# Weight units of the expert stages loaded in pairs of 1 MB instead of singly at 512 KB

## The reference

```python
def peer_ffn(xn, w_peer_q, sub_keys, expert_u, expert_v):
    ...
    best, pick = lax.top_k(cand, PEER_TOPK)
    expert_idx = jnp.take_along_axis(cand_idx, pick, axis=-1)
    gates = jax.nn.softmax(best, axis=-1)
    ...
    def step(args):
        xc, ic, gc = args
        u = expert_u[ic]
        hval = jnp.einsum('cd,chkd->chk', xc, u).astype(jnp.float32)
        a = (gc * jax.nn.gelu(hval, approximate=False)).astype(xc.dtype)
        return jnp.einsum('chk,chkd->cd', a, expert_v[ic])
```

## Time and profile before

| | us |
|---|---|
| three runs: median (lowest to highest) | 1323.77 (1323.52 to 1325.63) |
| span of the profiled execution | 1321.3 |
| PE busy | 1298.0 |
| DVE busy | 1067.7 |
| ACT busy | 818.5 |
| POOL busy | 215.6 |

### The profile page before, as it was taken

The page is one execution under the profiler, slowest core; times in us unless marked ns, Lnnn a source line. Parts: engine busy times, 40 slices in busy tenths (PEclk is TensorE's granted clock), DMA queues, the critical chain, the costliest instruction groups (busy, mean ns, idle before and its releaser), DMA issues.

```text
span 1321.3 us, 21738 instructions
## 1 busy us (share of the span) xinstructions
PE 1298.0 (98%) x8066; PEld 1199.7 (91%) x8066; DVE 1067.7 (81%) x1964; ACT 818.5 (62%) x1601; POOL 215.6 (16%) x153
## 2 busy tenths in 40 slices
PE   8999999999999999999999989999999999999998
PEld 6998888888889888889999989999989999999995
DVE  6867776666777675778999779999988898999985
ACT  6886555555556555455677688888665555555553
POOL 3002030000000000000000010110233444654510
PEclk9999999999999999999999999999999999999999
DMA  6534366565535345654566755566688999999982
GB/s 228 179 122 136 112 225 191 189 186 190 184 131 174 128 144 176 223 197 144 192 215 201 231 199 200 202 209 209 235 291 311 353 383 351 356 377 363 356 275 93
DMA packets 83135, 292.73 MB, mean 222 GB/s; under 512 B 10749, under 2 KB 11405, under 8 KB 82774
## 3 DMA queue, kind: packets, MB, share of 16 engines
q1 hardware_dynamic: 68182, 239.65, 53.1%
q0 software_dynamic: 14848, 51.69, 11.0%
HBM read 288.95 MB, written 2.34 MB: 220 GB/s over the span
## 4 chain that ended last, share of the span: by engine, by line
PE 80%; DVE 9%; DMA 5%; ACT 4%; issue 2%; POOL 0%; SPq 0%; POOLq 0%; ACTq 0%; DVEq 0%
PE bank L2404 78%; DMA raw<-in_wts 4%; DVE wl L661 3%; DVE rows L1599 1%; ACT wh L1743 1%; PE bank L2502 1%; PE bank L2490 1%; DMA rows<-in_u_rows,pick 1%; DVE oi L1576 0%; ACT oi L2324 0%; DVE gates L1631 0%; DVE gates L1584 0%; DVE oj L1572 0%; ACT oi L2328 0%; DVE us L1590 0%
## 5 line engine op out<-in xcount | busy, mean ns | idle before, releaser
L2404 PE MATMUL bank<-hTb,wh 128*128 128x416 f32 (+3 forms) x2768 | 826.8, 363 | 5.4 <-DVE wl L661 3.8
L2404 PE MATMUL bank<-hTb,wl 128*128 128x208 f32 (+2 forms) x2584 | 651.9, 264 | 0.0
L661 DVE TENSOR_TENSOR wl<-raw,wh 128x1024 fp32r<-128x1024 f32 x429 | 522.4, 1224 | 134.5 <-ACT wh L1743 133.1
L1743 ACT ACTIVATE wh<-raw 128x1024 fp32r<-128x1024 f32 x429 | 449.4, 1056 | 207.7 <-PE bank L2404 113.9
L2404 PEld LDWEIGHTS bank<-hTb,wh 128*128 128x128 f32 (+1 forms) x2768 | 505.5, 188 | 28.7 <-issue 6.7
L2404 PEld LDWEIGHTS bank<-hTb,wl 128*128 128x128 f32 (+1 forms) x2584 | 492.0, 190 | 4.8
L2404 PE MATMUL bank<-wh,hTb 128*128 128x512 f32 (+2 forms) x552 | 175.0, 398 | 1.4 <-DVE hTb L695 1.4
L2404 PEld LDWEIGHTS bank<-wh,hTb 128*128 128x128 f32 (+1 forms) x552 | 102.1, 186 | 24.3 <-DVE wl L661 1.6
L641 POOL DMA_INDIRECT rows<-in_v_rows,pick x48 | 95.9, 1998 | 92.5 <-DVE acc L1610 80.7
L641 POOL DMA_INDIRECT rows<-in_u_rows,pick x48 | 71.5, 1489 | 235.9 <-DVE dots L1599 231.7
L2404 PE MATMUL bank<-wl,hTb 128*128 128x512 f32 (+2 forms) x276 | 100.3, 389 | 0.0
(11 more groups left out here) (429 smaller groups left out, 1403.0 us busy)
## 6 DMA issues: line engine op xcount, KB each, us to landing
raw<-in_wts SPq DMA_DIRECT2D x441, 512.0 KB, 4.3
x<-in_x SPq DMA_DIRECT2D x4, 256.0 KB, 6.9
sk<-in_sk SPq DMA_DIRECT2D x1, 1024.0 KB, 6.8
spill<-x SPq DMA_DIRECT2D x1, 1024.0 KB, 7.6
xr<-few_x POOLq DMA_DIRECT2D x2, 512.0 KB, 12.3
x<-spill SPq DMA_DIRECT2D x4, 256.0 KB, 7.4
rows<-in_u_rows,pick POOLq DMA_INDIRECT x48, 7.5
rows<-in_v_rows,pick POOLq DMA_INDIRECT x48, 8.2
```

The lines of the kernel that those rows point to most:

```text
L661: e.tensor_tensor(b[:, :], raw[u % RAW][:, :], a[:, :].bitcast(F), ALU.subtract).then_inc(S("lo"), 1)
L1743: e.activation(parts_of(u)[0][:, :], raw[u % RAW][:, :], ACT.Copy).then_inc(S("hi"), 1)
L2404: return e.matmul(o, l, r, start=first, stop=last, skip_group_check=True)
```

## The change

From the first even unit of U on (186) up to unit 439, two units travel in one transfer. The host lays them side by side, so that each of the 128 partitions gets 8 KB in one piece. These 254 units make 127 transfers. The four buffers become four quarters of one tile `raws`, so that a pair fills two neighbouring ones: units 4k+2 and 4k+3 in the second half, 4k and 4k+1 in the first. Units 0 to 185 and unit 440 are loaded as before.

A pair's transfer is issued when the low steps of both units that held the half before are done: for even u, `lo` at least u-2, which is the end of unit u-3's low step. Before, unit u waited for the end of unit u-4's, and unit u+1 for that of u-3. Both units' high steps wait for the landing of the whole pair, on the semaphore of its first quarter; a table `landed` holds which semaphore and which count.

```diff
+def paired(units):
+    first = units.index(("U", ORDER[0]))
+    first += first % 2
+    return first, first + (len(units) - first) // 2 * 2
...
+        PAIRS, SINGLE = paired(units)
+        landings = [0] * RAW
+        landed = []
+        for u in range(len(units)):
+            slot = u % RAW
+            if PAIRS <= u < SINGLE:
+                slot -= u % 2
+            if not (PAIRS <= u < SINGLE and u % 2):
+                landings[slot] += 16
+            landed.append((f"raw{slot}", landings[slot]))
...
-        raw = [sb(f"raw{i}", [128, 1024]) for i in range(RAW)]
+        raws = sb("raws", [128, RAW * 1024])
+        raw = [raws[:, two(1024, i)] for i in range(RAW)]
...
             def weights(n):
                 for u in range(loaded[0], n):
+                    if PAIRS <= u < SINGLE:
+                        if u % 2 == 0:
+                            e.wait_ge(S("lo"), u - RAW + 2)
+                            e.dma_start(raws[:, 1024 * (u % RAW):1024 * (u % RAW) + 2048],
+                                        I["pairs"][(u - PAIRS) // 2]).then_inc(S(landed[u][0]), 16)
+                        continue
                     if u >= RAW:
                         e.wait_ge(S("lo"), u - RAW + 1)
-                    e.dma_start(raw[u % RAW][:, :], I["wts"][u]).then_inc(S(f"raw{u % RAW}"), 16)
+                    e.dma_start(raw[u % RAW], I["wts"][u - max(0, u - PAIRS)]).then_inc(S(landed[u][0]), 16)
...
-                    e.wait_ge(S(f"raw{u % RAW}"), 16 * (u // RAW + 1))
+                    e.wait_ge(S(landed[u][0]), landed[u][1])
```

More of the change, by code:

```diff
@@ L654, in low @@
                     if units[u][1] == "w_ple_gate":
-                        e.scalar_tensor_tensor(out=wl[u % SPL][:, :], in0=raw[u % RAW][:, :],
+                        e.scalar_tensor_tensor(out=wl[u % SPL][:, :], in0=raw[u % RAW],
                                                scalar=gpc[:, units[u][2]:units[u][2] + 1],
@@ L660, in low @@
                     a, b = parts_of(u)
-                    e.tensor_tensor(b[:, :], raw[u % RAW][:, :], a[:, :].bitcast(F), ALU.subtract).then_inc(S("lo"), 1)
+                    e.tensor_tensor(b[:, :], raw[u % RAW], a[:, :].bitcast(F), ALU.subtract).then_inc(S("lo"), 1)
                 lows[0] = max(lows[0], n + 1)
@@ L1739, in high @@
                             e.wait_ge(S("in_later"), 96)
-                        e.activation(wh[u % SPL][:, :], raw[u % RAW][:, :], ACT.Copy,
+                        e.activation(wh[u % SPL][:, :], raw[u % RAW], ACT.Copy,
                                      scale=gpc[:, k:k + 1]).then_inc(S("hi"), 1)
                         continue
-                    e.activation(parts_of(u)[0][:, :], raw[u % RAW][:, :], ACT.Copy).then_inc(S("hi"), 1)
+                    e.activation(parts_of(u)[0][:, :], raw[u % RAW], ACT.Copy).then_inc(S("hi"), 1)
                 highs[0] = max(highs[0], n + 1)
@@ L3261, in layout @@
     rows = lambda v: np.ascontiguousarray(np.broadcast_to(v.reshape(1, -1), (128, v.size)))
-    k = {"wts": w, "x": a["x"], "p": a["p"]}
+    first, end = paired(units)
+    k = {"wts": np.concatenate([w[:first], w[end:]]), "x": a["x"], "p": a["p"]}
+    k["pairs"] = np.ascontiguousarray(w[first:end].reshape(-1, 2, 128, 1024).transpose(0, 2, 1, 3)).reshape(-1, 128, 2048)
     k["fold"] = np.zeros((128, 2, 128), np.float32)
```

## The result

The changed kernel took 1403.38 us (median of 4 runs, 1396.40 to 1404.48), the kernel before, run beside it, 1323.64 us (4 runs, 1322.85 to 1325.63). The ratio on record is 1.0578 (not quite the quotient of the two medians, 1.0602), with a 95% interval of 1.0553 to 1.0604: **80 us slower**, where 21.5 us had been forecast and 1372 us was the upper end of the range. The direction was right, the size far off.

A forecast was written before the change was run, and what follows sets the result against it. PE was taken to bound the kernel, with the four-buffer loop close behind. V's loop of 5.3 + 4.95 us gave +20 us and the place near 760 us +1.5: 1323.8 + 21.5 = 1345 us, range 1321 to 1372 us.

The forecast's parts named there:

- the loop's slack of 0.9 us: In V before the change: issue, landing, high and low step take 8.7 us, against four PE units, 9.60 us.
- The engine part, 4.95 us: In V: from the even unit's high step through a use of gathered rows to the odd unit's low step's end.
- The slower loop sets the pace of both: In V: the buffer half with gathered rows between its low steps, 4.94 us against 3.74, paces both halves.
- The landing time D, 5.3 us: A pair's landing in V: 3.3 us alone, 1.4 for the second 512 KB, 0.6 for meeting gathers.
- it waits half of one: 0.8 x 0.75 = 0.6 us: In V: a pair finds the engines at a gather with 0.8 likelihood and waits half of its 1.5 us.
- The upper bound: D in V with a whole gather ahead, 6.2 us; today's landing plus the second half, 7.8 us, was not taken.
- Between 925 and 1047 us ... I count no gain: Last stretch before V and V's start: PE lacks 3.0 + 1.2 us today, loop about as long as needed, no change.
- The U stage: U, few or no gathers: loop 4.7 + 4.95 us against an allowed 10.1, cost nothing; 1 to 3 us could go.
- Near 760 us, +1.5: Around 760 us, where high steps wait for landings: the second late unit lands one unit's landing later, +1.5 us.
- The gates' stage, nothing: While gates are built: lateness of 1 to 2 us falls on ACT, cost nothing; rival with 13 us more, chance 0.08.
- Much slower: Rival for V: whole gather or rest of a pair ahead, D 6.2 us, +47 us, 1372 us; chance 0.13.
- The rule of the Trainium skill: It asks for at least 1 MiB per transfer; its 6.15 us as D gives 333 us in V, 1370 us in all.

The follow-up runs named there:

- experiment 5: The kernel before without its 96 gathers (POOL writes one column instead; the 48 other tokens' part is left out): 1320.61 us, ratio 0.9977.
- experiment 9: The changed kernel with V's uses of gathered rows (DVE) moved from between a pair's two low steps to behind the second: 1380.51 us, ratio 1.0420.
- experiment 4: The changed kernel with its 96 gathers replaced by a small fill on POOL (the 48 other tokens' results left out): 1340.50 us, ratio 1.0108.
- experiment 11: The kernel before with six places for single units from unit 297 to 391, two of them in `x`, which returns later: 1325.11 us, ratio 1.0001.
- experiment 6: The changed kernel with a third place for pairs in the space of `x`, units 298 to 391, and `x` brought back later: 1356.40 us, ratio 1.0224.
- experiment 8: The changed kernel with pairs that begin at odd units and buffers turned by one: 1393.78 us, ratio 1.0506.

## Why the prediction was wrong in size

Step by step, as the prediction put them.

- **What bounds the kernel; the loop's slack of 0.9 us.** Right. The slack carried single landings that gathers had stretched from under 4 to 6.4 us at a price of 3 us in all (experiment 5), and pairs used it up.
- **The engine part, 4.95 us.** Nearly right in V: 4.71. "The slower loop sets the pace of both" was too strict, the mean counts; experiment 9 shows each tenth of a microsecond in it coming back as 3 us in V (4.06 for 4.71 us: 0.65 / 4 x 120 = 20 us by the loop, with D's 0.18 another 5; 25 measured).
- **The landing time D, 5.3 us. This step failed.** Measured: 6.70 us. The unloaded part was 4.9 us, 0.2 above my 4.7. The term "it waits half of one: 0.8 x 0.75 = 0.6 us" was the error: gathers cost a pair 1.8 us, since without them D is 4.91 us (experiment 4). How, the 16 counts of each pair's semaphore show, if each is read as one engine that is done. On average the first count comes 4.55 us after the issue, the mean of the 16 at 5.13 and the last at 6.70; without gathers it is 4.34, 4.57 and 4.91. So the mean engine loses 0.56 us, and for it my 0.6 us was right. But a pair lands when the last engine is done, and with gathers the engines finish apart: from first to last count it is 2.1 us in the median pair and up to 5.6, without them 0.4. That is the other 1.2 us. I had a pair wait as if all engines kept in step; why they part, the runs don't show. The pairs fall into two groups: 18 of the 59 saw less than 0.95 of a gather's 128 pieces between issue and landing and took 4.82 us on average, the other 41 took 7.52. (A longer flight also sees more pieces, so this is no price of one gather.) The error is 1.4 / 4 x 120 = 42 us, less 7 us for the smaller engine part: 35 of the 58 us by which I missed.
- **The upper bound.** I refused today's landing plus the second half, 7.8 us, because "with pairs there is hardly one in front". True for weights: but the 6.4 us of before were also made of gathers. The landing of single units without them is 3.7 to 3.9 us (experiment 5), so 2.5 to 2.7 of the 3.1 us above's 3.3 were gathers. 6.70 us lies between 6.2 and 7.8, and a range to 7.8 us would have held the result: (7.8 + 4.95) / 4 x 120 = 382 us in V, 1420 us.
- **"Between 925 and 1047 us ... I count no gain"**, and no loss. This step failed too: 12.1 us were lost. For units 294 to 311 D was 6.48 us and the engine part 6.63, since the turn from U to V puts other steps of DVE between the low steps; 3.29 us a unit for 2.71 before. Without gathers the turn took 56.8 us with pairs, so 9.5 of the 12.1 us hang on them here too. I had used V's 4.95 us there, unmeasured. A row could have warned me: the stretch 925:1000 of the earlier trace rows, with DVE at 68.38 of 75 us, is not a place where a pair's two low steps stand close.
- **The U stage, "I cost it at nothing"**: 5.7 us. Here also the step failed. The sorting steps of DVE stand between the low steps of a pair, the engine part is 5.47 us and not 4.95, D 4.99, and 0.44 us pass between the two: 10.93 / 4 = 2.73 us a unit, for 2.61 that it took before and the 2.53 that I gave as PE's need. "The loop may take 10.1 us" was the right comparison with a wrong left side. The chain at 673 us shows it, in the changed kernel:

```profile
671.38 1.23 DVE wl L685
672.60 0.70 DVE bst L1442 x4
673.31 0.99 DVE pos__245 L1444 x4
674.30 1.13 DVE wl L685
...
675.45 4.51 DMA raws<-in_pairs
```

- **Near 760 us, +1.5**: 2.3 measured, but that shows little: kernels that are the same up to there differ by 2.8 us in this stretch (experiment 11), and experiment 6, whose pairs are the same there, took 26.3 us, less than before. A pair there took 15.23 us to land; whether the mechanism is the one I told stays open.

```profile
753.75 15.23 DMA raws<-in_pairs
```

- **The gates' stage, nothing**: 3.0 us (160.4 without gathers, as before), and 19 in the profiled run of experiment 8. I had named it as the place where I was least sure.
- **The sum**: 20 + 1.5 = 21.5 stood for 56.6 + 2.3 + 12.1 + 5.7 + 3.0 = 79.7 us. "Much slower", with a chance of 0.13, was the case that came, beyond its own 1372 us. Its D of 6.2 us was right within 0.5, though not by a whole gather ahead of every pair; it left out the stages ahead of V.
- **The rule of the Trainium skill** ("DMA: Bandwidth & Descriptors", sections "Bandwidth" and "Rules for kernel authors"): by its 6.15 us for 1 MB, measured there on transfers issued from GpSimd, the estimate in V was 333 us, against 342.6 measured, nearer than my 307.5. That was luck: a pair without gathers lands after 4.9 us here, and the rest is gathers. The full bandwidth that it promises for transfers of 1 MiB and more did not come: V moved 294 GB/s with them and 357 without, because the engines idled 20% of the time with no buffer to fill.

Of what I said would show it, DMA and low steps by turns in the chain did. PE's waits did in part: 36.4 us in 24 waits, not once per pair, and all but one on the gates' low part and not on a low step. D near 5.3 and V at 305 to 310 us failed by their size, and "up to 760 us nothing moved by more than 2 us" failed with the U stage's 5.7. Of what I said would be wrong, one thing came in part: 11 us of the loss sit before 940 us.

## What to carry to other kernels

With a fixed number of bytes for buffers, larger transfers mean fewer places: write down the loop (issue to landing, plus first use to last use of everything in the buffer), divide by the units in it, and compare with the consumer's pace *in every stage*, with the steps that stand between the uses in that stage. Take the landing time under the load that will be there: a buffer is full when the last engine is done, not the mean one, so half of what stands ahead is too little. Counting in full what may be met comes near here, though it is not how the loss arises (an estimate from the earlier trace rows and the 1.25 gathers a pair: 1.25 x 1.5 = 1.9 us, for 1.8 measured). If the loop is near the limit, the cheap cures are another place or uses that stand close together (here 47 and 23 us), not another shape of transfer.

## What the runs showed of the hardware

- With gathers of 128 rows of 4 KB on another queue, 1 MB lands 1.8 us later on average (6.70 us for 4.91), though the mean of the 16 engines is only 0.56 us later (5.13 for 4.57), if each count of the semaphore is one engine. The rest is the last engine's lag behind the mean.
- 1 MB without gathers lands after 4.8 us (median in V; 4.6 at the least) and 512 KB after 3.3 (median early in U; 3.0 at the least): the second half costs 1.5 to 1.6 us.
- A piece of 8 KB keeps an engine busy for 309 ns and one of 4 KB for 159 ns (medians), and with either the kernel took the same time (1403 and 1407 us).
- DMA transfers that keep their engines less busy can be what holds a kernel up: the busy share in V fell from 0.96 to 0.80 as their landings came into the loop that binds.
- The stretches' granted clock of 0.95 and 0.96 for 1.00 before is a mean of two levels. In V the clock stands at its upper level but for eight pieces of 3.4 us at the lower one, 1.2 GHz. The first begins at 1053.9 us, when PE had just waited 1.79 us and, 7 us earlier, 1.48 us; a matmul over 416 columns took 0.59 us in it, for 0.37 on either side:

```profile
1053.90:1057.30 3.40, 3.40 (x13) 3.30 (x14) 2.39 (x4) 0.00 (x0) 2.70 (x2) 0.50 0.45 130
```

  That had no part in the loss: the loop holds no step of PE, and its sum closes without it. The kernel before has such a piece too, at 768.6 us, which a slice of 33 us on its page does not show.
